# One core, two blocks in fp32r: the columns of each weight unit dealt out to four quarters, read by the matmuls in turn

## The reference

```python
h = rms_norm(x, g_mix); proj = h @ w_in
q, k, v, z, f, scal, gates = jnp.split(proj, SPLIT_POINTS, axis=-1)
y_a = gated_deltanet_branch(q, k, v, z, scal, ...)      # ends in @ w_up
y_f = fourier_branch(f, w_fourier)                      # ends in @ w_lin
gate_a, gate_f = jnp.split(jax.nn.sigmoid(gates), 2, axis=-1)
x = x + (gate_a * y_a + gate_f * y_f) @ w_o
h = rms_norm(x, g_mlp)
x = x + jnp.square(jax.nn.relu(h @ w_mlp_up)) @ w_mlp_down   # 2048 -> 8192 -> 2048
x = rms_norm(x, g_final)
```

## Time and profile before

| | |
|---|---|
| time, median of 2 runs | 2401.97 us (2401.75 to 2402.2) |
| the profiled execution's own time | 2400.65 us |
| its span, first to last instruction | 2398.9 us |
| mean granted TensorE clock | 0.998 |
| TensorE busy | 2372.5 us (99%), 12532 matmuls |
| VectorE busy | 1774.1 us (74%) |
| ScalarE busy | 1027.0 us (43%) |
| GpSimd busy | 266.7 us (11%) |
| loads and stores | 475.18 MB, 198 GB/s |

### The profile page before, as it was taken

How to read it: one execution, slowest core, us unless ns; L and a number is a source line. 1 busy time by engine, 2 the same in 40 slices (tenths; PEclk the granted TensorE clock), 3 DMA queues, 4 the chain that set the end, 5 groups by cost and what they waited for, 6 DMA issues and landing times.

```text
span 2398.9 us, 29924 instructions
## 1 busy us (share of the span) xinstructions
PE 2372.5 (99%) x12532; PEld 1943.8 (81%) x12532; DVE 1774.1 (74%) x2054; ACT 1027.0 (43%) x849; POOL 266.7 (11%) x226
## 2 busy tenths in 40 slices
PE   8999999999999999999999999999999999999998
PEld 7888788878888888888888888777777778888886
DVE  6585568467697887886766789989999967458865
ACT  5453345334344544444444435343434444544432
POOL 0002201210000000000000000056555400000000
PEclk9999999999999999999999999999999999999999
DMA  7343454347655555555555556665555586566753
GB/s 261 142 164 133 141 198 154 129 145 270 247 193 193 193 193 211 193 193 193 193 193 193 194 211 220 206 231 190 192 191 199 184 297 238 184 234 235 257 195 140
DMA packets 84230, 475.18 MB, mean 198 GB/s; under 512 B 8704, under 2 KB 8832, under 8 KB 32512
## 3 DMA queue, kind: packets, MB, share of 16 engines
q1 hardware_dynamic: 84096, 473.27, 55.7%
HBM read 450.17 MB, written 23.07 MB: 197 GB/s over the span
## 4 chain that ended last, share of the span: by engine, by line
PE 90%; DVE 6%; DMA 3%; issue 1%; ACT 1%; SPq 0%; DVEq 0%; ACTq 0%
PE acc L2180 28%; PE acc L2183 27%; PE acc L2186 27%; PE banks L2327 2%; DVE w_lo L1258 1%; PE banks L2376 1%; DMA raw<-in_w 1%; DVE convT L1578 1%; DVE padT L1305 1%; PE banks L2443 1%; PE banks L2456 1%; ACT w_hi L797 1%; DMA spilled<-stage 0%; PE banks L2197 0%; DMA c_in<-in_c_im 0%
## 5 line engine op out<-in xcount | busy, mean ns | idle before, releaser
L1258 DVE TENSOR_TENSOR w_lo<-raw,w_hi 128x2048 fp32r<-128x2048 f32 x394 | 909.4, 2310 | 380.0 <-ACT w_hi L797 376.9
L797 ACT ACTIVATE w_hi<-raw 128x2048 fp32r<-128x2048 f32 x394 | 752.8, 1915 | 669.4 <-DMA raw<-in_w 669.0
L2180 PE MATMUL acc<-w_hi,a_hi 128*128 128x512 f32 x2112 | 838.3, 397 | 6.4 <-DVE w_lo L1258 3.5
L2183 PE MATMUL acc<-w_lo,a_hi 128*128 128x512 f32 x2112 | 824.1, 390 | 0.0
L2186 PE MATMUL acc<-w_hi,a_lo 128*128 128x512 f32 x2112 | 823.7, 390 | 0.0
L2180 PEld LDWEIGHTS acc<-w_hi,a_hi 128*128 128x128 f32 x2112 | 396.9, 188 | 106.1 <-issue 16.9
L2186 PEld LDWEIGHTS acc<-w_hi,a_lo 128*128 128x128 f32 x2112 | 397.0, 188 | 84.7 <-DVE a_lo L1294 0.3
L2183 PEld LDWEIGHTS acc<-w_lo,a_hi 128*128 128x128 f32 x2112 | 397.2, 188 | 78.8
L2180 PE MATMUL acc<-w_hi,b_hi 128*128 128x512 f32 x928 | 361.7, 390 | 0.0
L2186 PE MATMUL acc<-w_hi,b_lo 128*128 128x512 f32 x928 | 361.1, 389 | 0.0
L2183 PE MATMUL acc<-w_lo,b_hi 128*128 128x512 f32 x928 | 361.0, 389 | 0.0
(11 more groups left out here) (354 smaller groups left out, 1681.6 us busy)
## 6 DMA issues: line engine op xcount, KB each, us to landing
raw<-in_w SPq DMA_DIRECT2D x395, 1024.0 KB, 4.8
spilled<-stage SPq DMA_DIRECT2D x72, 256.0 KB, 5.9
gate_in<-spilled SPq DMA_DIRECT2D x20, 512.0 KB, 5.9
x_rows<-in_x SPq DMA_DIRECT2D x4, 512.0 KB, 8.2
x_rows<-in_x SPq DMA_DIRECT2D x1, 2048.0 KB, 9.3
mem_rows<-in_mem SPq DMA_DIRECT2D x2, 1024.0 KB, 5.9
spilled<-stage_b SPq DMA_DIRECT2D x8, 256.0 KB, 6.0
out<-y_rows SPq DMA_DIRECT2D x3, 512.0 KB, 2.8
```

Of the source, the lines that this page charges most:

```text
L797: act.activation(w_hi[:, n % HIGH, :], raw[:, n % RAW, :], ACT.Copy)\
L1258: dve.tensor_tensor(w_lo[:, n % RAW, :], raw[:, n % RAW, :], w_hi[:, n % HIGH, :].bitcast(F32), ALU.subtract).then_inc(lo_split, 1)
L2180: pe.matmul(o, hi[:, tk], wh, start=first, stop=False)
L2183: pe.matmul(o, hi[:, tk], wl, start=False, stop=False)
```

## The change

It has two halves that belong together. On the host, `stream` splits the 512 columns of a K step into 128 groups of LANES = 4 and transposes these last two axes: in a partition, the 512 words of a K step now lie as four quarters of 128 words, and quarter z holds the columns 4j+z for j = 0 to 127. On the device, `moving` gives the matmul an access pattern over the same 512 words with the quarters innermost: word j of quarter 0, 1, 2, 3, then word j+1 of each. The array is fed with the columns in their natural order. Nothing else differs: loads, splits, results, waits and the order of instructions are those of before.

```diff
@@ -31,6 +31,7 @@
 NW = 512
 KU = 4
 UE = KU * NW
+LANES = 4
 RAW = 4
@@ -2172,8 +2173,8 @@
                     hi, lo = op(KU * u + k)
-                    wh = w_hi[:, n % HIGH, k * NW:(k + 1) * NW]
-                    wl = w_lo[:, n % RAW, k * NW:(k + 1) * NW]
+                    wh = moving(w_hi[:, n % HIGH, :], k)
+                    wl = moving(w_lo[:, n % RAW, :], k)
                     tk = slice(t * P, (t + 1) * P)
@@ -2546,10 +2547,15 @@
+def moving(x, k):
+
+    return x[:, k * NW:(k + 1) * NW].rearrange("p (z j) -> p j z", z=LANES)
+
+
 def stream(a):
 
     k, n = a.shape
-    return a.reshape(k // (KU * P), KU, P, n // NW, NW).transpose(3, 0, 2, 1, 4).reshape(-1, P, UE)
+    return a.reshape(k // (KU * P), KU, P, n // NW, NW // LANES, LANES).transpose(3, 0, 2, 1, 5, 4).reshape(-1, P, UE)
```

## The result

The changed kernel takes 2919.11 us (median of 2 runs, 2918.27 to 2919.96) against 2401.97 us, a ratio of 1.2158 with a 95% interval of 1.2128 to 1.2187. It is slower by 517 us, and its time is far under the forecast range of 4350 to 9550 us. The profiled execution spans 2916.5 us at a mean granted clock of 0.997.

A forecast was written before the change was run, and what follows sets the result against it. TensorE's 9504 weight matmuls were taken as the bound; a pitch of 858.2 ns instead of 226.7 added 9504 x 631.5 ns = 6002 us to 2400.65, so 8400 us. The 8-in-10 range was 4350 to 9550 us.

The forecast's parts named there:

- Slower, at 0.84: Whole kernel: chance given to a slower time; the same had 0.15, faster 0.01.
- One sign that I named: ScalarE's waits for loads, 669 us before, must turn into waits for TensorE.
- the 1.65 ns: Weight matmuls: time per isolated word, taken from VectorE's rows, giving a pitch of 858.2 ns and 8400 us.
- VectorE's tables of powers: State space branch: single words 64 bytes apart cost VectorE 1.48 to 1.83 ns instead of 1.045, runs of two nothing extra.
- nothing happens: Weight matmuls: TensorE's port holds or fetches ahead, pitch stays 226.7 ns and time 2400 us; chance 0.15.
- a hold of four places: TensorE's port: the point from which "nothing happens" decides; with fewer, each fetch is gone before its neighbour is asked for.
- 1.48 to 1.83 ns: VectorE's time per hopping element, least to most; carried to TensorE it gave 7576 to 9279 us.
- rival of the half rate: TensorE's port: a request brings two adjacent words per 0.833 ns, single words go at half rate, 440 ns, 4428 us; chance 0.23.
- as the columns lie now, what brings them from SBUF is at least as fast as the array: Weight matmuls before the change: the stream takes one column per cycle of the array at either clock level.
- the 0.01 for a gain: Whole kernel: chance of being faster by 2%; a gain was called all but excluded, with no conflict to resolve.
- the 13.4 ns over 213.3: Weight matmul pitch before: 226.7 ns against 213.3 for 512 columns at 2.4 GHz; 13.4 ns were "something else".
- My bound for that case, 2273 us: Weight matmuls: time if all of the 13.4 ns went, 2400.65 - 127 us.

The follow-up runs named there:

- The run in which one input alone hops: Kernel before, but only ScalarE's raw and VectorE's w_hi are read from two, four or 128 places by n % 4, all else adjacent: 2564.9 us.
- two halves: The change with LANES = 2, a word from each half of a K step in turn: 2317.0 us in five rounds, 0.9653 of the kernel before.
- two lines: The change with LANES = 2 and pieces of 4 words, places 16 bytes apart, order 0, 4, 1, 5, 2, 6, 3, 7: 2314.92 us.
- 0, 2, 1, 3: The change with LANES = 2 and pieces of 2 words, so only the order within 16 bytes differs from plain: 2400.63 us.
- fours from four quarters: The change with four adjacent words taken from each of four quarters in turn (LANES = 4, RUN = 4): 2773.58 us.
- 64 bytes: The change with LANES = 4 and pieces of 16 words, so the four places lie 64 bytes apart instead of 512: 2784.33 us.
- 2 KB: The change with LANES = 4 over the whole unit, four places 2 KB apart, longer waits for the first units: 2923.49 us.
- pairs from two halves: The change with two adjacent words taken from each of two halves in turn (LANES = 2, RUN = 2): 3416.7 us.
- 32 places: The change with LANES = 32, a word in turn from each of 32 pieces of 16 words: 4344.5 us.
- pairs from four: The change with two adjacent words taken from each of four quarters in turn (RUN = 2): 4443.86 us.
- every second word: Words of two K steps alternate in memory, a matmul reads every second word, always forward, longer waits for the first units: 4518.3 us.
- 8 places: The change with LANES = 8, a word in turn from each of eight pieces of 64 words: 4878.18 us.
- the first set: The change with only LANES altered to 2, 8 and 32, one execution each: 2318.2, 4878.18 and 4344.5 us.

## Why the prediction was wrong

**Right.** TensorE is the bound, and the change is worth 9504 times the difference of the pitch. The loads and the splits cost nothing (1912 and 2298 ns against 1915 and 2310). The clock didn't fall (0.997 against 0.998); the small matmuls of L2327 (now L2328) kept 220 ns. Slower, at 0.84. One sign that I named did not come: ScalarE's waits for loads didn't turn into waits for TensorE but grew. The next load is issued only when TensorE has done with a unit, and I read the growth as TensorE's slowness, seen there as a late load.

**The step that failed** is "I read the 1.65 ns as the time in which the memory serves one isolated word, whoever asks. [...] so it must be held up if VectorE is." No column of the change costs 1.65 ns: the pitch was 283.3 ns, 0.55 ns per column, and not 858.2. The first of two things that were missing between the rows of VectorE and TensorE is shown, the second argued.

*A word whose neighbour is asked for soon after costs less.* In VectorE's tables of powers no hop ever came back. The quarters come back after four columns. TensorE took 215.7 ns from two places, 283.3 from four and 486.7 from eight. The run in which one input alone hops shows the difference on VectorE itself: 1.17 ns per word (2389 / 2048) from two places, 1.95 (3985 / 2048) from four. This was my rival "nothing happens", to which I gave 0.15, with "a hold of four places" as its point; four places in turn don't come for nothing, on VectorE or on TensorE. The Trainium skill's line on a source that alternates between two regions at the full rate (Vector Engine (DVE) Microarchitecture Reference, section 5.2, Measured stream behaviour on trn2), quoted in the prediction as a mere rival, is for an operation with one source; with two sources here the 2389 ns are 3% over the plain 2325, so the trace nearly agrees. Four regions don't go as two do.

*TensorE behaves as if it had two readers, one for the even and one for the odd columns.* This is argued, not shown. A table of all orders by what one of these readers would do (words asked per fetch of four adjacent words, if it holds two places), in the order of the pitch:

| order | places per reader | words per fetch | pitch, ns |
|---|---|---|---|
| two halves; two lines | 1 | 4 | 215.7; 215.7 |
| plain; 0, 2, 1, 3 | 1 | 2 | 226.7; 226.7 |
| fours from four quarters | 4, one after the other | 2 | 267.9 |
| four quarters (the change); 64 bytes; 2 KB | 2 in turn | 4 | 283.3; 268.7; 283.3 |
| pairs from two halves | 2 in turn | 2 | 340.0 |
| 32 places; pairs from four; every second word; 8 places | no return in time | 1 | 433.0; 443.5; 451.4; 486.7 |

The groups don't overlap, but the two middle columns don't forecast their order: fours from four quarters have the words per fetch of the plain order and cost 41 ns more, and less than the change, whose fetches serve more words. With one word per fetch a reader would need 433.0 / 256 = 1.69 ns per word at 32 places, and 1.90 at eight (486.7 / 256). That is near my 1.48 to 1.83 ns, and near VectorE's 1.84 (3765 / 2048) and ScalarE's 1.87 (3835 / 2048) for 128 places. So the price of a lone word may have been right for TensorE too, if two readers share the columns. My rival of the half rate, 440 ns, stands as near to the 433.0 and 443.5 ns; these runs don't part the two. Had I seen the two readers and not the hold, the forecast would have been 512 x 1.65 / 2 + 13.4 = 436 ns and some 4400 us, right for 32 places; it is the early return to the neighbours that parts the change's 2919 from that.

**A second, smaller step failed:** "as the columns lie now, what brings them from SBUF is at least as fast as the array", and with it the 0.01 for a gain. Of the 13.4 ns over 213.3, 11 are the price of the plain order; in the order 0, 4, 1, 5, 2, 6, 3, 7 only 2.4 are left (215.7). My bound for that case, 2273 us, stands beside 2317. That the opening shows 427 ns without a surplus wasn't evidence for it: the change's opening shows no surplus either, and later it has one of 70 ns.

**What is shown and what is argued.** Shown: the dependence on the number of places, and hardly on distance among 64 bytes, 512 bytes and 2 KB; that the order within 32 bytes matters (215.7 against 226.7) and the order 0, 2, 1, 3 doesn't; that pairs from two halves are far worse than single words. That there are two readers is the simplest account I found, put before all but the first set. It forecast 216 (measured 215.7), 283 (283.3), and in direction 433 (451.4) and 283 (268.7), and it missed 283 (340.0) and 440, or 227 counted rightly (267.9). Open: whether the distances, all multiples of 64 bytes, add to the price of four places; why two places in turn for each reader cost TensorE 283 ns and not 216, if they are held (ScalarE's 2419 against 1913 is of the same kind); why 64 bytes are 15 ns better than 512; why eight places are worse than 32; and why a stretch of the change ran at 0.27 us. So the step that failed is known, and the size of 283 ns is not explained. A run in which each reader goes through four places but takes four words at each would test the account further.

## What to carry to other kernels

A price per access measured in one order doesn't carry to another order, nor to another engine, without its pattern of return: ask which words have a neighbour that is asked for soon after, and how many places lie between. For fp32r matmuls bound by their moving operand, lay the words so that four even columns are adjacent to each other, and four odd ones too (order 0, 4, 1, 5, 2, 6, 3, 7 or two halves): it is a permutation of the weights on the host and one access pattern, and it was worth 3.5% here. Don't let such an operand have a step of two words, or four places or more in turn: the least that either cost here was 41 ns per matmul.

## What the hardware showed that I hadn't expected

- The plain order isn't the fastest: 226.7 ns for 512 fp32r columns, and 215.7 from two places in turn.
- With a step of two words (8 bytes) a matmul takes 451.4 ns, twice as long, and with pairs of adjacent words from four quarters, the runs of two that are free on VectorE in the earlier trace rows, 443.5.
- VectorE and ScalarE read one input from two places in 2389 and 2419 ns per 2048 words and from four in 3985 and 3971; with an alternating output as well, ScalarE has 3979 from two.
